# Convolution stage of a hybrid decoder step: five gate units at the end, the next gated product ahead of GpSimd's last addition, the last chunk summed by TensorE, the last four squares one by one

## What is computed

```python
def conv_mixer(x, prev, norm_g, w_in, conv_w, conv_b, ln_g, ln_b, w_out):
    h = rms_norm(x, norm_g)
    a, b, z = jnp.split(h @ w_in, 3, axis=-1)
    u = a * jax.nn.sigmoid(b)
    u_ext = jnp.concatenate([prev.astype(u.dtype), u], axis=1)
    c = lax.conv_general_dilated(u_ext, conv_w[:, None, :], ...,   # causal, depthwise, width 31
                                 feature_group_count=E_A) + conv_b
    c = jax.nn.silu(layer_norm(c, ln_g, ln_b))
    out = (c * jax.nn.silu(z)) @ w_out
    return out, u_ext[:, -(CONV_W - 1):]
```

## Time and profile before

| | us |
|---|---|
| median of three runs | 2424.27 |
| the three runs | 2417.22, 2424.27, 2424.91 |
| the profiled execution | 2416.76 |
| its span | 2414.9 |
| PE, DVE, ACT, POOL busy over the span | 2209.6, 1313.2, 940.2, 1069.7 |
| mean granted clock of PE | 0.965 of full |

### The profile page before, as it was taken

How to read it: one execution, slowest core, us unless ns; L and a number is a source line. 1 busy time by engine, 2 the same in 40 slices (tenths; PEclk the granted TensorE clock), 3 DMA queues, 4 the chain that set the end, 5 groups by cost and what they waited for, 6 DMA issues and landing times.

```text
span 2414.9 us, 46942 instructions
## 1 busy us (share of the span) xinstructions
PE 2209.6 (91%) x16540; PEld 1908.8 (79%) x16540; DVE 1313.2 (54%) x1892; ACT 940.2 (39%) x1617; POOL 1069.7 (44%) x715
## 2 busy tenths in 40 slices
PE   5999999999458997979999999988999998989999
PEld 3999999999347997978999888854555555558998
DVE  4698889889874005574787311113544544545332
ACT  4566566556453003231322112323454444453121
POOL 0688998898766123443333343222222222212130
PEclk7999999999789998989999999988999999999999
DMA  3222222222124112131422579999999999973212
GB/s 114 69 71 76 67 70 76 74 66 76 58 74 163 50 52 87 61 133 66 150 74 89 203 243 335 357 358 397 415 397 397 417 397 397 405 298 113 65 45 84
DMA packets 137489, 430.99 MB, mean 178 GB/s; under 512 B 23889, under 2 KB 40658, under 8 KB 136162
## 3 DMA queue, kind: packets, MB, share of 16 engines
q1 hardware_dynamic: 121554, 375.94, 42.1%
q0 software_dynamic: 13168, 41.58, 4.8%
q10 hardware_dynamic: 2592, 11.14, 1.2%
HBM read 386.81 MB, written 43.87 MB: 178 GB/s over the span
## 4 chain that ended last, share of the span: by engine, by line
PE 53%; POOL 14%; DVE 8%; issue 8%; DMA 6%; ACT 6%; SPq 4%; ACTq 0%; POOLq 0%; DVEq 0%
POOL ACC L1371 7%; PE PS L611 6%; PE PS L613 6%; PE PS L612 6%; PE PS L728 5%; PE PS L730 5%; PE PS L729 5%; PE PS L850 4%; PE PS L794 3%; DMA KV<-cv 3%; POOL WL L1344 2%; PE PS L929 2%; PE PS L619 2%; DMA KV<-ck 2%; SPq L526 2%
## 5 line engine op out<-in xcount | busy, mean ns | idle before, releaser
L1344 POOL TENSOR_TENSOR WL<-RAW,WH 128x1024 fp32r<-128x1024 f32 (+1 forms) x121 | 305.3, 2525 | 575.3 <-ACT WH L979 570.7
L1687 DVE SCALAR_TENSOR_TENSOR PS<-UX,CWT,PS 128x1024 f32<-128x1024 f32 (+1 forms) x672 | 466.3, 782 | 0.0
L644 PE MATMUL PS<-HH,WH 128*128 128x384 f32 (+1 forms) x1152 | 378.5, 329 | 20.7 <-DVE HL L1673 20.7
L646 PE MATMUL PS<-HH,WL 128*128 128x384 f32 (+1 forms) x1152 | 377.4, 328 | 0.0
L645 PE MATMUL PS<-HL,WH 128*128 128x384 f32 (+1 forms) x1152 | 377.2, 327 | 0.0
L1371 POOL TENSOR_TENSOR ACC<-ACC,PROD 128x1088 f32<-128x1088 f32 x112 | 284.7, 2542 | 31.3 <-ACT PROD L1031 25.1
L728 PE MATMUL PS<-GH,WH 128*128 128x384 f32 (+1 forms) x792 | 267.0, 337 | 24.2 <-DVE KC L1812 12.1
L730 PE MATMUL PS<-GH,WL 128*128 128x384 f32 (+1 forms) x792 | 262.5, 331 | 0.0
L729 PE MATMUL PS<-GL,WH 128*128 128x384 f32 (+1 forms) x792 | 261.4, 330 | 0.0
L644 PEld LDWEIGHTS PS<-HH,WH 128*128 128x128 f32 x1152 | 217.3, 189 | 24.7 <-issue 13.7
L979 ACT ACTIVATE WH<-RAW 128x1024 fp32r<-128x1024 f32 (+1 forms) x121 | 131.3, 1086 | 241.8 <-PE PS L613 207.5
(11 more groups left out here) (220 smaller groups left out, 4338.7 us busy)
## 6 DMA issues: line engine op xcount, KB each, us to landing
KV<-ck SPq DMA_DIRECT2D x256, 512.0 KB, 12.2
KV<-cv SPq DMA_DIRECT2D x256, 512.0 KB, 12.6
RAW<-wA SPq DMA_DIRECT2D x48, 512.0 KB, 3.4
RAW<-wP SPq DMA_DIRECT2D x16, 640.0 KB, 4.0
zT_scr<-ZS ACTq DMA_DIRECT2D x16, 544.0 KB, 2.7
Z<-zT_scr SPq DMA_DIRECT2D x16, 544.0 KB, 3.7
RAW<-wB SPq DMA_DIRECT2D x17, 512.0 KB, 3.4
RAW<-wO SPq DMA_DIRECT2D x16, 512.0 KB, 3.5
```

What stands on the lines that cost most here:

```text
L644: pe.matmul(out, WH[w][:, kk], HH[:, k, a:b], start=k == 0, stop=False)
L646: mm = pe.matmul(out, WL[w][:, kk], HH[:, k, a:b], start=False, stop=k == KD - 1)
L1344: pool.tensor_tensor(WL[s][:, 0:n], RAW[s][:, 0:n], WH[s][:, 0:n].bitcast(F32), ALU.subtract).then_inc(s_lo, 1)
L1687: i = dve.scalar_tensor_tensor(out=o, in0=x, scalar=w[:, j:j + 1], in1=o, op0=ALU.mult, op1=ALU.add)
```

## The change

The order of the units is now a list, `conv_order`: b and a of each chunk as before, but z units lag. After a of chunks 0, 4, 8, 12 and 15 no z unit follows, so that z of chunk 0 comes after a of chunk 1, and so on, and the z units of chunks 11 to 15 stand at the end. Banks are taken in rotation over five. All loops of this stage are written out. On ACT, POOL and SP the number of units handled in a chunk is now three, or two in chunks 0, 4, 8 and 12. POOL's `gated(n + 1)` moves into chunk n, ahead of its last addition. SP issues all `raw` loads of a chunk first and then the twelve page copies. The last chunk is no longer added by POOL to the sum; PE adds it to the mean in a second group of products. The squares of chunks 12 to 15 are summed by PE one by one.

```diff
-        SLOT_BANK = ((0, 1, 2), (3, 4, 0), (1, 2, 3))
-        SLOT_BACK = (4, 4, 4, 4, 9, 5, 5, 5, 5)
+        Z_WAITS = (0, 4, 8, 12, 15)
+        conv_order = []
+        for n in range(NCH):
+            conv_order += [(n, 0), (n, 1)]
+            if n not in Z_WAITS:
+                conv_order.append((n - sum(w < n for w in Z_WAITS), 2))
+        conv_order += [(n, 2) for n in range(NCH - len(Z_WAITS), NCH)]
+        place = {x: u for u, x in enumerate(conv_order)}
+        a_place = [place[n, 1] for n in range(NCH)]
+        MEAN = PS[:, 0:3, :].rearrange("p a n -> p (a n)")[:, 0:R]
...
+        def slot_bank(g):
+            return g % 5
...
# SP
-                for j in (5, 6, 7):
-                    u = 3 * n + j
-                    if not (isinstance(u, int) and u == U_OUT + 4):
...
-                    past_logf(i, NPG // 2 * s + 4 * (j - 5), 4)
+                for u in range(a_place[n] + 4, a_place[n + 1] + 4 if n < NCH - 1 else U_OUT + 4):
+                    conv_raw(u)
+                for j in range(3):
+                    past_logf(n // 2, NPG // 2 * s + 4 * j, 4)
...
# PE
+            for u, (n, kind) in enumerate(conv_order):
+                pe.wait_ge(s_lo, u + 1)
+                for r, (a, b) in enumerate(RCH):
+                    g = 3 * u + r
+                    atleast(pe, s_eva, max(g - 4, 6) if u == PAIRED > 0 and r > 0 else g - 4)
...
-            pe.wait_ge(s_csum, NCH + 1)
+            pe.wait_ge(s_csum, NCH)
             pe.wait_ge(s_eva, 9 * NCH)
+            mean_part(CSUM, True)
             pe.wait_ge(s_c, NCH)
-            for a, b in ((0, 512), (512, 1024), (1024, R)):
-                mm = pe.matmul(CHAIN[:, a:b], ONES, CSUM[:, a:b], start=True, stop=True)
-            mm.then_inc(s_mmu, 1)
-            for p in range(NCH // 2):
+            mean_part(CC[:, NCH - 1, :], False).then_inc(s_mmu, 1)
+            for p in range(6):
                 pe.wait_ge(s_sqp, p + 1)
-                colsum(pe, 0, SQ1[2 * (p % 2)], p == 0, p == NCH // 2 - 1).then_inc(s_var, 1)
+                colsum(pe, 1, SQ1[2 * (p % 2)], p == 0, False).then_inc(s_var, 1)
+            for n in range(12, NCH):
+                pe.wait_ge(s_sq1, n + 1)
+                colsum(pe, 1, SQ1[n % 4], False, n == NCH - 1).then_inc(s_var, 1)
...
# ACT, in place of chunk(n, s, i); empty(u, r) is sigmoid_b, copy_a or silu_z by the unit's kind
+            for n in range(NCH):
+                s, u = n % 2, a_place[n] + 1
+                three = n == NCH - 1 or a_place[n + 1] == u + 2
+                conv_hi(u + 1)
                 product(n, s, 0)
                 product(n, s, 1)
+                empty(u, 0)
                 product(n, s, 2)
+                empty(u, 1)
                 product(n, s, 3)
+                empty(u, 2)
+                conv_hi(u + 2)
                 product(n, s, 4)
+                if three:
...
+                else:
+                    product(n, s, 5)
+                    product(n, s, 6)
+                    empty(u + 1, 0)
+                    product(n, s, 7)
+                    empty(u + 1, 1)
+                    empty(u + 1, 2)
+                    product(n, s, 8)
+            for u in (U_OUT - 2, U_OUT - 1):
+                conv_hi(u + 1)
+                for r in range(3):
+                    empty(u, r)
+            conv_hi(U_OUT + 1)
...
# POOL
-                gated(n, s)
-                lo(3 * n + 3, (s + 3) % 2)
+            gated(0, 0)
+            for n in range(NCH):
+                s, u = n % 2, a_place[n] + 1
+                lo(u + 1, (u + 1) % 2)
+                if n > 0:
                     csum(n - 1)
                 adds(n, s, range(1, 3))
+                lo(u + 2, (u + 2) % 2)
                 adds(n, s, range(3, 6))
+                if n == NCH - 1 or a_place[n + 1] == u + 2:
+                    lo(u + 3, (u + 3) % 2)
+                adds(n, s, range(6, NT - 1))
+                if n < NCH - 1:
+                    gated(n + 1, 1 - s)
+                adds(n, s, range(NT - 1, NT))
+            for u in range(U_OUT - 1, U_OUT + 2):
+                lo(u, u % 2)
-            csum(NCH - 1)
-            for p in range(NCH // 2):
+            for p in range(6):
```

More of the change, by code:

```diff
@@ L627, in _ @@
                 colsum(pe, 1, T0[k % 2], k == 0, k == KD - 1).then_inc(s_st0, 1)
[L629 to L647, removed]
@@ L649, in _ @@
-            paired(pe, NCH, chunk)
-            pe.wait_ge(s_csum, NCH + 1)
+            for u, (n, kind) in enumerate(conv_order):
+                if u < PAIRED:
+                    continue
+                pe.wait_ge(s_lo, u + 1)
+                for r, (a, b) in enumerate(RCH):
+                    g = 3 * u + r
+                    atleast(pe, s_eva, max(g - 4, 6) if u == PAIRED > 0 and r > 0 else g - 4)
+                    if g == 3:
+                        pe.wait_ge(s_sd0, 1)
+                    out = PS[:, slot_bank(g), 0:b - a]
+                    for k in range(KD):
+                        if g == 0:
+                            pe.wait_ge(s_h, k + 1)
+                        kk = slice(k * P, (k + 1) * P)
+                        pe.matmul(out, WH[u % 2][:, kk], HH[:, k, a:b], start=k == 0, stop=False)
+                        pe.matmul(out, WH[u % 2][:, kk], HL[:, k, a:b], start=False, stop=False)
+                        mm = pe.matmul(out, WL[u % 2][:, kk], HH[:, k, a:b], start=False, stop=k == KD - 1)
+                    mm.then_inc(s_slot, 1)
@@ L651, in _, with mean_part @@
+            def mean_part(src, first):
+                for a, b in PAIR_CH:
+                    mm = pe.matmul(MEAN[:, a:b], ONES, src[:, a:b], start=first, stop=not first)
+                return mm
+            pe.wait_ge(s_csum, NCH)
             pe.wait_ge(s_eva, 9 * NCH)
+            mean_part(CSUM, True)
             pe.wait_ge(s_c, NCH)
-            for a, b in ((0, 512), (512, 1024), (1024, R)):
-                mm = pe.matmul(CHAIN[:, a:b], ONES, CSUM[:, a:b], start=True, stop=True)
@@ L1020, in silu_z, with conv_hi, empty @@
                 act.wait_ge(s_slot, slots(n, 2) + r + 1)
-                act.activation(ZS[:, a:b], PS[:, SLOT_BANK[2][r], 0:b - a], ACT.Silu).then_inc(s_eva, 1)
+                act.activation(ZS[:, a:b], PS[:, slot_bank(slots(n, 2) + r), 0:b - a], ACT.Silu).then_inc(s_eva, 1)
+                if r == 2:
+                    act.wait_ge(s_eva, slots(n, 2) + 3)
+                    act.dma_start(zT[n], ZS[:]).then_inc(s_zst, 16)
+            def conv_hi(u):
+                hi(u, u // 2, u % 2, conv=True)
+            def empty(u, r):
+                n, kind = conv_order[u]
+                if kind == 0:
+                    sigmoid_b(n, n % 2, n // 2 + 1, r)
+                elif kind == 1:
+                    copy_a(n, r)
+                else:
+                    silu_z(n, r)
             def product(n, s, q):
@@ L1049, in chunk @@
                 product(n, s, 2)
-                silu_z(n, 1)
+                empty(u, 1)
                 product(n, s, 3)
[L1052 to L1055, removed]
+                empty(u, 2)
+                conv_hi(u + 2)
                 product(n, s, 4)
-                if last:
-                    for q in range(5, NT):
-                        product(n, s, q)
-                    return
```

82 lines of the change are left out of this document (36 added, 46 removed).

## The result

The changed kernel takes 2441.35 us (median of 6 runs, 2438.68 to 2446.79); the kernel before, measured beside it, 2419.62 us (6 runs, 2412.36 to 2424.91). The ratio is 1.0096, 95% interval 1.0082 to 1.0109: slower, by 22 to 23 us. The profiled execution took 2440.9 us with a span of 2439.1, so 24.2 us more span than before.

The account below looks back on a forecast made before the run. PE looked like the bound, with POOL's own pace only 0.3 us a chunk behind. +23.8 to the mean's end and +1.1 for squares gave +24.9 on 2416.76, so 2441.7; the median was given as 2446, range 2420 to 2460.

Parts of the forecast that it names:

- Three-unit chunks, 35.3 a chunk from POOL's own pace: Convolution chunks with three units: POOL sets 35.3 us, so each saves 0.27 from 35.58.
- Chunk 0, 28.2: First two-unit chunk: SP is on time, `cw` lands before product 2 is due, `gated` of chunk 1 ends at 107.1.
- Two-unit chunks with SP, 39.95: Chunks 4, 8, 12: late `cw` holds ACT's product 2, adding 7.8 us to 32.15, so 4.4 longer than now.
- forecast lag of 13.3: SP's twelve page copies end 13.3 us into the next chunk, and its stores and the `cw` load come only then.
- The wait of ACT for `cw`: Sign in chunks 4, 8 and 12: ACT waits 7 to 9 us for the DMA of `cw` ahead of `sigmoid_b`.
- Two-unit chunks without SP, 32.15: Convolution: one `lo` less, a smaller ACT gap and earlier `hi` take 3.15 us off POOL's 35.3.
- rival A: SP not late or nobody waits: two-unit chunks 32.15, yet no change, 2418.3 or 2425.8 us on the median; chance 0.16.
- The last slot emptied at 670.9, the mean at 675.0: End of convolution: five z units run until 670.4, ACT empties by 670.9, mean ends at 675.0 against 651.2, +23.8.
- Squares +1.1: After the mean: four squares summed singly by PE in place of pairs add 1.1 us, bounds +0.5 and +1.5.
- Rival B: Convolution: POOL's gaps close once PE is early, chunks run at DVE's 32; about 2397, or 2404 on median; chance 0.11.
- Rival C: Idle PE in two-unit chunks falls to half clock, costing +8: 2450, or 2454 us on the median; chance 0.13.
- The rule against the row: SP's page copies: the skill calls DMA initiation time small; the prediction followed the trace instead, 1.59 us apiece, 20.5 for twelve.

Follow-up runs that it names:

- e4: e1 with the `gated` product back at the start of its chunk on POOL; 2418.84 us, ratio 1.0007 to the kernel before.
- e1: Changed kernel with SP copying four pages behind each `raw` load again, in place of twelve behind the last; 2415.44 us, ratio 0.9994 to the kernel before.
- e2: Changed kernel with four of the twelve page copies ahead of the chunk's third `raw` load, eight behind the last; 2422.41 us (one run).
- e7: e3 with the twelve page copies behind the last `raw` load again, as in the change; 2409.37 us (one run).
- e3: e1 with only the z units of chunks 0, 8 and 15 waiting, so three z units at the end; 2404.44 us, ratio 0.9946.
- e6: e3 with only chunk 0 a two-unit chunk, so two z units at the end; 2407.06 us, ratio 0.9949.
- e8: e3 with all sixteen squares summed by PE one by one and no POOL additions of squares; 2399.86 us, ratio 0.9922.
- e9: e3 with the last chunk added by POOL to the sum again and one group of products for the mean; 2403.58 us (one run).

## Why the prediction was right, point by point

- **Three-unit chunks, 35.3 a chunk from POOL's own pace:** 35.15. Right; the difference is the chain of additions that the moved `gated` breaks (e4, 0.18 a chunk).
- **Chunk 0, 28.2:** 28.5. The start of the last `gated` was forecast at 613.2 (615.4 less its 2.23) and came at 613.23; small errors cancelled: eleven chunks 0.15 to 0.35 shorter, three 0.05 to 1.4 longer, and chunk 0 0.2 longer. That the sum meets the measured start so closely is luck.
- **Two-unit chunks with SP, 39.95:** 40.56, 41.35, 40.0. The mechanism is shown three ways: taken away (e1, 32.27), dosed (e2), and on a single chunk (e7). The forecast lag of 13.3 was 13.9, 15.2 and 13.9. The term was sized 0.05 to 1.4 low; the copies took 19.7 to 20.96 us, and `cw` landed 2.3 (median) after its issue instead of 1.9. The wait of ACT for `cw`, named as a sign at 7 to 9 us, was 13.95 in chunk 4: it starts when ACT is done with product 1, while the 7.8 of the sum counts only from when product 2 was due.
- **Two-unit chunks without SP, 32.15 (rival A):** 32.27 in e1, and the time of rival A, no change, is what e1 gave. So even the step that was only argued, that nothing is won since PE gets its z units back at the end, holds. Only its place was off: in e1 PE's idle time falls in the chunk behind the two-unit chunk.
- **The last slot emptied at 670.9, the mean at 675.0:** 671.0 and 675.2. Right.
- **Squares +1.1:** +2.0, above the upper bound of 1.5. This is the step that was mis-sized. Single sums cost 0.4, less than the 1.1; the other 1.6 is the half clock of the second pair, which the sum had at nothing. "Its gap before it remains" spoke of the first pair only. e7 shows that this stretch can also stay away, so it belonged into the bounds and not into the middle of the sum.
- **Rival B** (POOL follows PE down to 32) is refuted: the gaps of 1.50 and 0.94 to 1.00 stay in the three-unit chunks of every variant, none of which took less than 34.9 us. In two-unit chunks the second gap is 0.45.
- **Rival C** (PE's clock) is real in the record but not in the time of the chunks (what it cost came in the squares): PE ran at half for 3 to 10 us in chunks 4, 5, 8, 9, 12 and 13, and `gated` waited for ACT's copy of a only once, in front of chunk 0 (the waits above). The row it was taken from holds for the first products behind an idle time here as well: 4.00 instead of 2.10 for the first sum of squares.
- **The rule against the row:** the sentence of the Trainium skill (DMA: Bandwidth & Descriptors, "Issuing engines are not separate DMA queues") that the time to initiate a DMA "is usually small relative to the DMA itself" does not hold for this loop of copies. Twelve took SP 19.7 us in the rows of SP above, 1.64 each, against a median of 2.0 from issue to landing, and moving them back was worth the whole loss (e1). The DMA instruction itself is 0.54 of the 1.64 (median); the rest goes with the loop and the page number read in front of it.

The sum was 2441.7 against a profiled execution of 2440.9; the forecast of 2446 leaned on the higher level of the three runs then known, and the median is 2441.35.

What the expectation for e3 rested on, two equations, also says what the change should have been: each two-unit chunk gives DVE and POOL about 3 us and costs PE 11.86 at the end, of which the 25.6 us tail has room for two. Four moved units (e1) overshoot it, two (e3) fit, one (e6) leaves PE as the bound from chunk 8 on. Three were not run.

## What to carry to other kernels

Before freeing the busiest engine, take its waits out of the next engine's timeline and read what pace is left: here it was 0.3 us away, and the relief ended there. When an order is rewritten, go through the queue engines as through the compute engines: here a small copy with its address read first held its queue for 1.6 us, and twelve in a row in front of one small load that an in-order engine needs early cost 8 to 9 us each time. Work moved into a tail must be counted against the tail's length (25.6 us, two units of 11.86), and its effect on PE's clock belongs into the sum, as bounds: here the squares took 0.3 to 3.1 us more than before.

## What the runs showed of the hardware that I had not expected

PE's clock can cost a short stage several us in a way that the rows ahead of it don't tell. In front of the first sum of squares PE was idle 6.3 us in every kernel but e8, and that sum took 3.5 to 4.0 us instead of 2.10. Behind a mean at half clock (one group of 4.01 us in the kernel before and of 3.90 in e9, two of 4.07 and 4.09 in e6) no later sum did, and the stretch was 34.9 to 35.4 us. Behind a mean at full clock there were more half-clock stretches and it took 36.6 to 38.1 us in six kernels, but in e7 it took 35.4. e3 and e7 run the same instructions there, with the same idle times up to the first sum. So the link with the mean's clock is not shown as a cause, and whether the stretch also differs between executions of one kernel was not measured. Keeping PE without idle time among the squares (e8) left half clock only in the first two sums.

Two POOL additions of 128x1088 stand 2.63 to 2.69 us apart when the second needs the result of the first (2.63 in the kernel before, 429.63 - 427.00; 2.69 in the changed one), and 2.48 to 2.51 when it does not or when other work follows.
